# One projected tile moved ahead of an index stage, and values turned in two PSUM banks where keys take four

## The reference

```python
z = n @ w_in                       # 5192 columns: conv GLU | q | k | v | indexer q, k, head weights | gates
q, k, qi, ki = rotary of their columns
# index scores, on queries t and keys s
I[t, s] = sum_h w[t, h] * relu(qi[t, h] . ki[s])
# prompt: the 256 best admissible keys; sample: the 65 best of 256 cached + 4 new keys (pages by page_table)
att = softmax(q . k_kept / 8) @ v_kept
# conv branch: GLU -> causal depthwise conv (31 taps) -> LayerNorm -> silu -> W_conv_out
h = h + g2 * (sigmoid(g_c) * conv_out + sigmoid(g_a) * att @ W_attn_o) @ W_out
```

## Time and profile before

| | |
|---|---|
| Median of 3 runs | 2723.54 us (2717.31 to 2726.49) |
| The profiled execution, own time | 2726.95 us |
| Its span in the trace | 2724.6 us |
| TensorE matmuls, busy | 2552.8 us (94%) |
| VectorE busy | 1302.6 us (48%) |
| ScalarE busy | 598.7 us (22%) |
| GpSimd busy | 918.6 us (34%) |
| Granted TensorE clock, mean | 0.965 of full speed |

### The profile page before, as it was taken

How to read it: one execution, slowest core, us unless ns; L and a number is a source line. 1 busy time by engine, 2 the same in 40 slices (tenths; PEclk the granted TensorE clock), 3 DMA queues, 4 the chain that set the end, 5 groups by cost and what they waited for, 6 DMA issues and landing times.

```text
span 2724.6 us, 41950 instructions
## 1 busy us (share of the span) xinstructions
PE 2552.8 (94%) x15990; PEld 2372.9 (87%) x15990; DVE 1302.6 (48%) x2420; ACT 598.7 (22%) x1079; POOL 918.6 (34%) x490
## 2 busy tenths in 40 slices
PE   5999999999999878899998769899899999999998
PEld 3899999999998846799997436889799999999997
DVE  4333333333334637799998345451533333333333
ACT  2310011101102323312334367310401111001103
POOL 1123323322233225546997010123133333333332
PEclk8999999999999979999999869999999999999999
DMA  8322222222220522221225500343011111111111
GB/s 278 109 78 77 70 77 77 69 69 77 77 77 21 149 76 72 77 97 48 87 94 169 180 1 1 95 136 100 16 47 47 44 44 44 45 46 46 46 54 64
DMA packets 208658, 209.93 MB, mean 77 GB/s; under 512 B 14143, under 2 KB 161715, under 8 KB 207657
## 3 DMA queue, kind: packets, MB, share of 16 engines
q1 hardware_dynamic: 198380, 181.70, 21.1%
q10 hardware_dynamic: 10181, 26.90, 3.1%
HBM read 173.03 MB, written 28.94 MB: 74 GB/s over the span
## 4 chain that ended last, share of the span: by engine, by line
PE 72%; DVE 18%; issue 4%; ACT 3%; SPq 2%; DMA 1%; POOL 1%; DVEq 0%; ACTq 0%; POOLq 0%
PE main L248 21%; PE main L249 21%; PE main L250 21%; DVE junk L1128 6%; DVE aux L1333 3%; DVE pick L1282 2%; PE main L1684 1%; PE main L1701 1%; PE aux L1712 1%; SPq L1467 1%; PE aux L983 1%; PE main L336 1%; PE aux L336 1%; ACT tmp L452 1%; PE aux L394 1%
## 5 line engine op out<-in xcount | busy, mean ns | idle before, releaser
L248 PE MATMUL main<-nhi,whi 128*128 128x352 f32 x3192 | 1042.5, 327 | 23.4 <-DVE nlo L464 20.0
L249 PE MATMUL main<-nlo,whi 128*128 128x352 f32 x3192 | 1029.2, 322 | 0.0
L250 PE MATMUL main<-nhi,wlo 128*128 128x352 f32 x3192 | 1028.2, 322 | 0.0
L235 POOL CAST whi<-raw 128x1024 fp32r<-128x1024 f32 x185 | 196.7, 1063 | 1586.7 <-PE main L250 1271.4
L248 PEld LDWEIGHTS main<-nhi,whi 128*128 128x128 f32 x3192 | 602.5, 189 | 56.6 <-issue 44.0
L249 PEld LDWEIGHTS main<-nlo,whi 128*128 128x128 f32 x3192 | 603.6, 189 | 0.6
L250 PEld LDWEIGHTS main<-nhi,wlo 128*128 128x128 f32 x3192 | 602.0, 189 | 0.6
L237 POOL TENSOR_TENSOR wlo<-raw,whi 128x1024 fp32r<-128x1024 f32 x185 | 461.7, 2496 | 14.8
L686 DVE TENSOR_TENSOR tmp<-main,tmp 128x352 f32<-128x352 f32 x132 | 69.3, 525 | 779.5 <-PE main L250 776.4
L705 DVE SCALAR_TENSOR_TENSOR h<-main,ada,h 128x352 f32<-128x352 f32 (+1 forms) x528 | 296.8, 569 | 114.7 <-PE main L250 114.7
L248 PE MATMUL main<-hid_hi,whi 128*128 128x352 f32 x1056 | 342.8, 325 | 0.0
(11 more groups left out here) (300 smaller groups left out, 2413.3 us busy)
## 6 DMA issues: line engine op xcount, KB each, us to landing
ada_raw<-in_w_ada SPq DMA_DIRECT2D x18, 2048.0 KB, 9.4
raw<-in_w_gate SPq DMA_DIRECT2D x44, 512.0 KB, 3.7
raw<-in_w_up SPq DMA_DIRECT2D x44, 512.0 KB, 3.8
raw<-in_w_down SPq DMA_DIRECT2D x44, 512.0 KB, 3.6
raw<-in_w_in SPq DMA_DIRECT2D x40, 512.0 KB, 3.6
gate_d<-zraw ACTq DMA_DIRECT2D x16, 528.0 KB, 2.7
gates<-gate_d SPq DMA_DIRECT2D x16, 528.0 KB, 4.6
zsw<-zraw ACTq DMA_DIRECT2D x42, 132.0 KB, 2.4
```

The costliest lines, as they stand in the source:

```text
L235: pool.tensor_copy(hi, raw[:, slot]).then_inc(hi_done, 1)
L248: pe.matmul(bank, w_hi[:, w], hi(c), start=(i == 0), stop=False)
L249: pe.matmul(bank, w_hi[:, w], lo(c), start=False, stop=False)
L250: last = pe.matmul(bank, w_lo[:, w], hi(c), start=False, stop=(i == n - 1))
```

## The change

Two things, in one diff.

First, tile 5 (`Z_Q`, the first 128 columns of the queries) is computed by TensorE directly after tile 4, ahead of the index stage, and SyncE loads its weights directly after those of tile 4, ahead of the rotary table and the pages. ScalarE copies it out and issues its four swap DMAs ahead of its part of the index stage, after the same wait for the rotary product of tile 4 as before. TensorE's wait ahead of the turned state is now for tile 5's banks. The scores of the prompt move on by one tile: from tiles 5 and on to tiles 6 and on.

Second, the values (groups 0 to 8) and the first group of keys are turned in banks main 2 and main 3 alone, so the wait for `CV_TOTAL` ahead of the values goes; a turn waits for ScalarE's copy of the group two before it. From group 10 (the second of the keys) the cycle of four banks stands as before, and ahead of group 10 there is a wait for `CV_TOTAL - LEFT`. The wait for `CV_TOTAL` ahead of the LayerNorm's sums was there and stays.

```diff
@@ piece_at
-            n = 2 * (6 * (L - Z_Q) + 2 * t + half)
-            return range(n, n + 2) if L >= Z_Q and n < len(PIECES) else range(0)
+            n = 2 * (6 * (L - Z_Q - 1) + 2 * t + half)
+            return range(n, n + 2) if L > Z_Q and n < len(PIECES) else range(0)
@@ m1_sp
-            for L in range(3, Z_Q):
-                load_tile(sp, T_Z + L, L % RING, cols(w_in, ZCOL[L]))
+            for L in range(3, Z_Q + 1):
+                load_tile(sp, T_Z + L, (T_Z + L) % RING, cols(w_in, ZCOL[L]))
...
-            for L in range(Z_Q, NZ):
+            for L in range(Z_Q + 1, NZ):
                 load_tile(sp, T_Z + L, L % RING, cols(w_in, ZCOL[L]))
@@ m1_pe
             for L in range(2, Z_Q):
                 z_product(pe, L, T_Z + L, L % RING, 3 * L, L % 2)
 
-            pe.wait_ge(z_free, 6 + 3 * Z_Q)
+            z_product(pe, Z_Q, T_Z + Z_Q, (T_Z + Z_Q) % RING, 3 * Z_Q, Z_Q % 2)
+            pe.wait_ge(z_free, 6 + 3 * Z_Q + 3)
             pe.wait_ge(state_in, 32)
...
-            for L in range(Z_Q, Z_LOOP):
+            for L in range(Z_Q + 1, Z_LOOP):
@@ m1_act
                     act.dma_start(ki_b[HD:P, :], kiw[0:HD, :]).then_inc(kib_in, 16)
+            act.wait_ge(rope_a, 3 * Z_Q)
+            evac(act, zrow(Z_Q), Z_Q, ACT.Copy, None)
+            act.wait_ge(z_free, 6 + 3 * Z_Q + 3)
+            swap(act, Z_Q, P)
             for g in range(2):
                 act.wait_ge(st_t, g + 1)
...
-            act.wait_ge(rope_a, 3 * Z_Q)
-            for L in range(Z_Q, Z_GLU):
+            for L in range(Z_Q + 1, Z_GLU):
@@ turn_bank
         def turn_bank(g):
+            if g < 9:
+                return main[:, 2 + g % 2]
             return (main[:, 2], main[:, 3], aux[:, 0], aux[:, 1])[g % 4]
@@ turn_tokens
-                if g >= 4:
-                    pe.wait_ge(kv_e, g - 3)
+                if g >= 2:
+                    pe.wait_ge(kv_e, g - 1 if g < 10 else g - 3)
+                if g == 10:
+                    pe.wait_ge(cv, CV_TOTAL - LEFT)
@@ m2_pe
             pe.wait_ge(v_in, 16)
-            pe.wait_ge(cv, CV_TOTAL)
             for t in range(9):
                 turn_tokens(t, vraw, t)
```

## The result

| | before | after | ratio, 95% interval |
|---|---|---|---|
| first comparison, medians of 4 and 4 runs | 2721.20 us | 2702.91 us (2701.43 to 2706.54) | 0.9934 [0.9917, 0.9951] |
| the same again, 24 and 6 runs | 2718.84 us | 2705.54 us | 0.9946 [0.9929, 0.9964] |
| the profiled execution, own time | 2726.95 us | 2706.54 us | |
| its span | 2724.6 us | 2704.3 us | |

The account below looks back on a forecast made before the run. VectorE's chain was taken as the bound to 1509 us, then the value pages. TensorE's 7.2 us at the index stage became 7.6 at the keys and value product: 2715.9 us median, own range 2713 to 2719, widened 2707 to 2723.

Parts of the forecast that it names:

- Tile 5 in the shadow of the wait: Before the index stage: 11.4 us of matmuls fill the wait, first index product 4.2 us later, TensorE gains 7.2 us.
- The rival that the clock stays up: Index stage: no gap as long as 13.88 us, so full clock; 9 us more gain, 2707 us; chance 0.12.
- The scores move whole; the projections after them are TensorE's own, so TensorE reaches `m2` 7.2 us earlier: Index stage's end to m2: the scores shift unchanged, so the 7.2 us gain carries through to m2.
- VectorE's chain "4.2 us later": Threshold search and convolution: ends at 1513.3, free by over 10 us at key group 10, 19 at LayerNorm's sums.
- The values and the banks: Value turns: vraw lands at 1497.8, nine groups take 8.4 us; two banks cost 1.4, start 11.3 earlier, 9.9 net.
- Logits: Sequences 2 to 7, 15.4 us: low clock at the start loses 2.3 us; keys start 7.6 us earlier.
- Value pages: Before L1659's second half: pages issued 9.0 us earlier, last lands 1553.3; TensorE's chain, 1554.5, decides by little.
- Slower, by the clock at the logits: Value turns through logits: clock stays low, logits lose 13.1 us; 9 us slower, 2733 us; chance 0.08.
- Both waits go whole: Waits for qib and last convolution tap: 13.9 + 16.9 = 31 us gained, 2693 us; chance 0.05.
- Only tile 5's part comes out short: Rotary product ends at 973.5 or logits lose 5 us: gain 5 us, 2718.5; chance 0.20 with last rival.
- the change does nothing here: m2: vraw binds as CV_TOTAL did, SyncE's pages fill the rest; 0 to -3 us; chance 0.20 with first rival.
- The signs of being wrong: First index product past 980.7, value turns past 1501, clock 0.50 past 1515, or any wait on L1317 or L1336.

Follow-up runs that it names:

- after_again: The changed kernel, unaltered, measured and traced once more: 2705.54 us, ratio 0.9946 to before.
- banks_only: The kernel before with the second part of the change alone (values turned in two banks): 2715.17 us, ratio 0.9990.
- quiet_sign: First part alone, plus a wait holding GpSimd's rotary product of tile 12 until VectorE's sign multiplications are done: 2717.85 us, ratio 0.9988 to before.
- pool_quiet: Changed kernel with GpSimd issuing vraw and value pages of sequences 4 to 7, and waiting for VectorE's sign multiplications: 2705.53 us, ratio 0.9931 to before.

## Why the prediction was wrong, point by point

- *Tile 5 in the shadow of the wait: right.* The rotary product ended 12.3 us behind T4 in after (0.5 ahead of the early end that the prediction kept, 970.7), 14.0 in after_again; 13.3 was forecast. The first index product came 19.9 us behind T4 in the mean of three traces where it had come 16.3: 3.6 us later, forecast 4.2. The clock was at 0.50 in the stage, as forecast, and the stage took 19.7 us. TensorE gains 11.4 - 3.6 = 7.8 us, forecast 7.2. The rival that the clock stays up fell.
- *"The scores move whole; the projections after them are TensorE's own, so TensorE reaches `m2` 7.2 us earlier": this step failed first.* From T4 to z end the gain was 11.3 us. The other 3.6 us lie in the scores: from the stage's end to the threshold the traces of after are 4.5 us shorter in the mean, and some of that is given back behind it. Most of it is the clock's. The windows over just that stretch, of before, banks_only, after and after_again:

```profile
993.76:1141.23 147.47, 133.04 (x655) 97.14 (x656) 105.54 (x111) 55.04 (x100) 69.23 (x30) 0.93 0.23 62
```

```profile
986.15:1130.09 143.94, 129.54 (x648) 94.93 (x649) 105.65 (x112) 55.05 (x100) 69.30 (x30) 0.95 0.24 64
```

```profile
992.68:1135.62 142.94, 129.21 (x648) 94.09 (x649) 105.27 (x111) 54.72 (x100) 69.02 (x30) 0.95 0.25 68
```

```profile
998.72:1141.16 142.44, 127.75 (x655) 93.54 (x656) 105.29 (x111) 54.95 (x100) 69.24 (x30) 0.97 0.25 68
```

  Length times clock is 137.1, 136.7, 135.8 and 138.2 us: the same within 2.4 us, with no order by kernel. Some 1.4 of these 2.4 can be the rounding of the clock. What goes with the length is the time lost to the low level: 10.3 us in before, 7.2 in banks_only, 7.1 and 4.3 in the two of after. In windows of 2 us it shows, apart from the first us behind the stage, as short drops to 0.50 of some 3.4 us each, which begin at the end of one of TensorE's waits for `rbuf` or up to 1.3 us behind it. Before has five such waits over 2 us and four drops, after four and three, after_again five and one. So the drops stand at waits, but their number differs between executions of one code. banks_only has before's code in that stretch, and three drops. Whether the shift of the scores against the splits also makes drops rarer stays open: the ten traces with tile 5 ahead lost between 2.8 (quiet_sign, 0.98 over 139.4 us) and 8.8 us in this stretch, the three without it 7.2, 10.3 and 10.3. Over all of them the gain from T4 to z end is 10.2 us, not 11.3, so the 3.6 us are uncertain by more than 1 us.
- *VectorE's chain "4.2 us later", slack 17 to 19 us: wrong by far, without consequence for the time.* From T4 it ended 11.5 us later in the mean, 562.4 where it had been 550.9. Of this 3.6 are the later stage, 12.4 the signs' multiplications and what follows them (380.2 less 367.8), and -4.5 the shorter stretch above. At the sums 6.1 us were left (19 forecast), ahead of group 10 1513.31 - 1510.85 = 2.5 us ("free by over 10 us"). The prediction priced what the change moves on TensorE and took the durations of VectorE's operations as fixed. The first part alone was made slower by this and by the later stage, 7.2 and 4.9 us.
- *The values and the banks: right.* `vraw` ended the wait 29.2 us behind z end (29.6 forecast), and the nine groups took 8.46 us (8.4).
- *Logits: this term was mis-sized.* 2.3 us of loss were forecast, 0 were measured: 1512.82 - 1497.44 = 15.4 us, as at full clock before. The 5 us of half clock were there in after's trace, but all of them in the turns, which ScalarE paces anyway; at 1494 the clock was back. Keys came 3.0 us earlier against z end than before (1531.47 - 1475.44 = 56.0 us, now 53.0), not 0.4.
- *Value pages: the other branch decided.* With no loss at the logits TensorE's chain was ready first, and the pages bound, by 0.5 to 1.65 us; they came 1.5 us earlier against z end (1.8 forecast). Together this part gave 86.3 - 84.8 = 1.5 us, forecast 0.4.
- *The sum.* 7.8 + 3.6 + 1.5 = 12.9 us, forecast 7.6: 0.6 more from the stage, 3.6 from the clock in the scores, 1.1 from the logits and the pages. The other 5.4 us of the first comparison were not placed; the scatter of T4 and of the time behind the stretch is of that size. The prediction gave the scores no term at all, so its range had no room for one.
- *The rivals.* "Slower, by the clock at the logits" fell: no loss there. Only pool_quiet shows its mechanism, and small: 1.2 us at the logits, behind a stall of 3 us, where the rival had 13.1. "Both waits go whole" fell: 4.0 + 2.2 and 11.2 us are left of them. "Only tile 5's part comes out short" and "the change does nothing here" fell with the 7.8 us of the stage.
- *The signs of being wrong.* None of those named came: no first index product later than 980.7 (22.8 us behind T4; 21.1 at most), no value turns later than 1501, no low clock past 1515, no wait for the convolution. They all looked for a loss, and the forecast failed by a gain.

The Trainium skill, SBUF — State Buffer, section "SBUF: two separate sides", has the port pair of VectorE and GpSimd as a lock held for a whole instruction. The trace agrees in the rows above, where five operations of 0.4 to 0.7 us grew to 1.3 to 2.9 us each beside GpSimd's of 1.3 to 2.8, and quiet_sign shows it by taking GpSimd away. The prediction had used that rule for one rotary product and not for the chain that followed.

## What to carry to other kernels

When a change shifts one engine's work by a tile, look at every short operation of VectorE that runs in a gap of GpSimd's work, and price it both alone and in turns with GpSimd: here 3.06 and 12.6 us for the same six operations, 9.6 us more, where the shift itself gained 7.8. Two edits of which one brings work forward and the other removes the wait behind it must be measured together: alone they gave +8 to 9 us and nothing that could be told from zero, together -13 or more. And compare traces from a point ahead of the change: 10 us of scatter sat in front of it.

## What the runs showed of the hardware that was not expected

- Six operations of VectorE on 1024 columns took 3.06, 9.7, 10.5 or 12.6 us, by GpSimd's phase beside them; 9.7 came in a trace whose code up to there was that of the 3.06; a wait of 3.9 us on GpSimd brought them back to 3.06.
- The granted clock fell to 1.2 GHz for some 3.4 us at or just behind the end of some waits of 2.0 to 2.5 us, while others of that length in the same stretch went without it; the number of these drops differed between executions of one kernel (three and one in after's). Each loses 1.7 us of clock (half of 3.4).
- In the value turns, where TensorE was paced to one group in 1.01 to 1.04 us by ScalarE, the clock came back all the same after 5 us in after's trace; with a stall of 3 us in them, in pool_quiet, it was back for good only after 14.
- SyncE's first page after a bulk load comes late: 7.3 us from the end of the issue behind `vraw`'s (1482.06) to the first key page in after (1489.40), while in the run of 16 value pages one takes 2.6 us. GpSimd's queue issued the same pages at 2.8 us each.
